# An expert stage whose tokens travel by indirect transfers, with each tile's down product behind the next tile's up products

## The reference

```python
logits = (t @ w_router).astype(F32)
top_v, top_i = lax.top_k(logits, TOP_K)
top_w = jax.nn.softmax(top_v, axis=-1)
gates = jnp.sum(jax.nn.one_hot(top_i, N_EXPERTS) * top_w[..., None], axis=-2)
for e in range(N_EXPERTS):
    out = out + gates[:, e:e + 1] * swiglu(t, w1[e], w3[e], w2[e])
```

## Time and profile before

| | |
|---|---|
| median of 3 runs | 1569.56 us (1569.21 to 1571.90) |
| the profiled execution, its time | 1572.87 us |
| its span | 1571.1 us |
| TensorE busy | 1453.8 us, 93% |
| VectorE busy | 1096.3 us, 70% |
| ScalarE busy | 769.8 us, 49% |
| moved by DMA | 318.02 MB |

### The profile page before, as it was taken

How to read it: one execution, slowest core, us unless ns; L and a number is a source line. 1 busy time by engine, 2 the same in 40 slices (tenths; PEclk the granted TensorE clock), 3 DMA queues, 4 the chain that set the end, 5 groups by cost and what they waited for, 6 DMA issues and landing times.

```text
span 1571.1 us, 19887 instructions
## 1 busy us (share of the span) xinstructions
PE 1453.8 (93%) x7153; PEld 1172.1 (75%) x7153; DVE 1096.3 (70%) x1423; ACT 769.8 (49%) x795; POOL 38.1 (2%) x61
## 2 busy tenths in 40 slices
PE   4999879999999977999999679999999999999996
PEld 1884446999999866778877457787877877877874
DVE  2686975334343467788888648788787787887786
ACT  2420254213222245465655247676676676665662
POOL 1000000000000011000000100000000000000000
PEclk7999989999999987999999879999999999999998
DMA  9888266443433322222223108797897887987971
GB/s 354 306 315 329 107 210 243 167 134 107 133 114 107 106 71 89 85 70 64 83 88 100 55 27 298 274 363 274 280 341 279 304 327 275 349 289 271 350 289 73
DMA packets 136277, 318.02 MB, mean 202 GB/s; under 512 B 5951, under 2 KB 42119, under 8 KB 130087
## 3 DMA queue, kind: packets, MB, share of 16 engines
q1 hardware_dynamic: 132992, 310.14, 55.8%
q0 software_dynamic: 2384, 5.54, 1.1%
q10 hardware_dynamic: 855, 1.74, 0.3%
HBM read 315.63 MB, written 1.77 MB: 202 GB/s over the span
## 4 chain that ended last, share of the span: by engine, by line
PE 80%; DVE 10%; ACT 5%; issue 3%; DVEq 0%; ACTq 0%
PE ps L263 22%; PE ps L265 22%; PE ps L264 22%; DVE v L872 3%; PE ps L1721 3%; PE ps L1606 2%; DVE wl L247 2%; ACT wh L241 2%; PE ps L1332 1%; PE ps L1637 1%; PE ps L1378 1%; PE ps L1610 1%; DVE x L349 1%; DVE yacc L1260 1%; DVE xn L348 1%
## 5 line engine op out<-in xcount | busy, mean ns | idle before, releaser
L247 DVE TENSOR_TENSOR wl<-raw,wh 128x2048 fp32r<-128x2048 f32 x253 | 575.3, 2288 | 150.0 <-ACT wh L241 149.6
L241 ACT ACTIVATE wh<-raw 128x2048 fp32r<-128x2048 f32 x253 | 483.8, 1916 | 292.9 <-PE ps L265 246.7
L263 PE MATMUL ps<-wh,xgh 128*128 128x512 f32 x480 | 193.6, 403 | 10.1 <-DVE yacc L1260 5.1
L265 PE MATMUL ps<-wh,xgl 128*128 128x512 f32 x480 | 190.3, 396 | 0.0
L264 PE MATMUL ps<-wl,xgh 128*128 128x512 f32 x480 | 190.2, 396 | 0.0
L263 PE MATMUL ps<-hTh,wh 128*128 128x384 f32 x480 | 164.6, 343 | 0.0
L264 PE MATMUL ps<-hTl,wh 128*128 128x384 f32 x480 | 163.1, 340 | 0.0
L265 PE MATMUL ps<-hTh,wl 128*128 128x384 f32 x480 | 163.0, 340 | 0.0
L263 PEld LDWEIGHTS ps<-wh,xgh 128*128 128x128 f32 x480 | 90.4, 188 | 35.9 <-issue 8.1
L265 PEld LDWEIGHTS ps<-wh,xgl 128*128 128x128 f32 x480 | 90.4, 188 | 22.0
L264 PEld LDWEIGHTS ps<-wl,xgh 128*128 128x128 f32 x480 | 90.5, 189 | 20.3
(11 more groups left out here) (287 smaller groups left out, 2312.7 us busy)
## 6 DMA issues: line engine op xcount, KB each, us to landing
raw<-in_moe_w SPq DMA_DIRECT2D x180, 1024.0 KB, 6.0
raw<-in_ada_w SPq DMA_DIRECT2D x48, 1024.0 KB, 6.8
raw<-in_ffn_w SPq DMA_DIRECT2D x33, 1024.0 KB, 5.6
raw<-in_conv_pw SPq DMA_DIRECT2D x12, 1024.0 KB, 12.1
raw<-in_mla_wo SPq DMA_DIRECT2D x8, 1024.0 KB, 4.8
raw<-in_mla_wuq SPq DMA_DIRECT2D x8, 768.0 KB, 4.7
gate<-gates_dram POOLq DMA_DIRECT2D x8, 512.0 KB, 4.9
raw<-in_mla_wukv SPq DMA_DIRECT2D x8, 512.0 KB, 3.7
```

The lines of the kernel that those rows point to most:

```text
L241: act.activation(wh[:, split_no(s) % HL, :], raw[:, s % RAW, :], ACT.Copy).then_inc(hi_made, 1)
L247: eng.tensor_tensor(wl[:, split_no(s) % HL, :], raw[:, s % RAW, :], wh[:, split_no(s) % HL, :], ALU.subtract).then_inc(lo_made, 1)
L263: nc.tensor.matmul(out_, sh, mh, start=start, stop=False)
L265: return nc.tensor.matmul(out_, sl, mh, start=False, stop=stop)
```

## The change

* The tokens no longer pass through `sel` in every tile. Two tables in memory, `xs_dram` and `ys_dram`, have a row for each place of 14 tiles. GpSimd writes each token's row to its two places by indirect DMAs (three blocks of tokens, twice), SP loads a tile's 128 rows into `xrow`, and TensorE turns them in eight transposes (`turn_rows_in`). Only tile 0 is still gathered by matmuls. A tile's output goes from PSUM through `ybuf` to `ys_dram`, by a DMA that ScalarE issues (`y_out`). After the last tile, six indirect DMAs bring each token's two rows back, and VectorE weighs and adds them. Scatter, `selT`, `yh`, `yl` and `G` are gone.
* Both tables are filled with zeros in the FFN stage: 28 DMAs of 128 rows, issued by GpSimd. ScalarE waits for them before the norm of the mla stage, since they read `hf`.
* The weights are read as rows of 8 KB. So partition p holds the inputs 8p to 8p + 7, and ScalarE writes `xn` in that order; hidden units are dealt four to a partition, and the product on VectorE writes `hm` in that order. A tile's up chunks are now all of w1 (chunks 0 to 5, banks 0 to 2), then all of w3 (6 to 11, banks 3 to 5). Silu is one instruction over 1536 columns, and the three products stand together.
* The loop is shifted. A turn holds the up chunks of tile e + 1 and the down chunks of tile e; the transposes of the hidden product lie between the first up chunks. Ahead of the loop are 12 up chunks of tile 0, behind it 6 down chunks of the last tile.
* The routing on VectorE makes row numbers (`rows_of`) for the transfers in place of the later tiles' `R` and `G`, in about as many steps.

```diff
+        xs_dram = nc.dram_tensor("xs_dram", [NT * P, D], F32, kind="Internal").ap()
+        ys_dram = nc.dram_tensor("ys_dram", [NT * P, D], F32, kind="Internal").ap()
...
+            ew1, ew3 = (d[n][0].rearrange("e (p k) n -> p e (k n)", k=DK) for n in ("moe_w1", "moe_w3"))
+            ew2 = d["moe_w2"][0].rearrange("e (g p j) n -> p e g (j n)", g=NG, j=4)
...
+            def load_next(e, up_of, down_of, static=False):
+                L = None if static else (e, TILE_CH)
+                load_up(NEXT, ew1, up_of, L)
+                sp.wait_ge(sem("xg_turned"), at(1, None if static else (e, 1)))
+                sp.dma_start(xrow[:, :], xs_dram[2 * P:3 * P, :] if static else xs_dram[ds(e * P + 2 * P, P), :])\
+                    .then_inc(sem("xrow_in"), 16)
+                load_up(NEXT + UP, ew3, up_of, L)
+                load_down(NEXT + 2 * UP, down_of, L)
...
+            load_up(MOE, ew1, 0)
+            load_up(MOE + UP, ew3, 0)
+            sp.wait_ge(sem("dispatched"), 16 * TC * TOP_K)
+            sp.dma_start(xrow[:, :], xs_dram[P:2 * P, :]).then_inc(sem("xrow_in"), 16)
...
+            blank = hf[:, :, :].rearrange("p k t -> p (k t)")[:, 0:D]
+            pool.memset(blank, 0.0).then_inc(sem("blank_made"), 1)
+            pool.wait_ge(sem("blank_made"), 1)
+            for t in range(NT):
+                for table in (xs_dram, ys_dram):
+                    pool.dma_start(table[t * P:(t + 1) * P, :], blank).then_inc(sem("tables_blank"), 16)
+            pool.wait_ge(sem("tables_blank"), 32 * NT)
...
+            pool.wait_ge(sem("rows_made"), 1)
+            pool.wait_ge(sem("tok_made"), TC)
+            for i in range(TOP_K):
+                for c in range(TC):
+                    pool.indirect_dma_start(out=xs_dram[:, :], out_offset=bass.IndirectOffsetOnAxis(ap=rows_of[:, c, i:i + 1], axis=0),
+                                            in_=xn[:, c, :], in_offset=None).then_inc(sem("dispatched"), 16)
...
+            pool.wait_ge(sem("y_last"), 16)
+            for c in range(TC):
+                for i, dst in enumerate((yacc, xn)):
+                    pool.indirect_dma_start(out=dst[:, c, :], out_offset=None, in_=ys_dram[:, :],
+                                            in_offset=bass.IndirectOffsetOnAxis(ap=rows_of[:, c, i:i + 1], axis=0))\
...
+            act.wait_ge(sem("tables_blank"), 32 * NT)
...
+                act.activation(xn[:, c, :].rearrange("p (k b a) -> p b a k", k=DK, b=DK),
+                               ps[:, 2 * c:2 * c + 2, :].rearrange("p u (b a k) -> p (u b) a k", b=DK // 2, k=DK), ACT.Copy)\
...
+            def silu(s, loop):
+                act.wait_ge(chunk_used, at(s, loop))
+                act.activation(ms[:, :, :], ps[:, 0:NG, :], ACT.Silu).then_inc(sem("ms_made"), 1)
...
+            for k in range(2 * UP):
+                make_hi(act, MOE + k + 3)
+                if k == UP:
+                    silu(MOE + UP, None)
+                if k == 11:
+                    rows_hi(xgh[:, :, :], (sem("xg_turned"), 1))
...
+            def y_out(e, s, static, signal):
+                L = None if static else (e, TILE_CH)
+                act.wait_ge(chunk_used, at(s, L))
+                if not static:
+                    act.wait_ge(sem("y_stored"), at(0, (e, 16)))
+                act.activation(ybuf[:, :], ps[:, 6:8, :].rearrange("p a b -> p (a b)"), ACT.Copy).then_inc(sem("y_copied"), 1)
+                act.wait_ge(sem("y_copied"), at(2, None if static else (e, 1)))
+                act.dma_start(ys_dram[0:P, :] if static else ys_dram[ds(e * P, P), :], ybuf[:, :]).then_inc(signal, 16)
+            def tile(e, static=False):
+                L, L1, L3 = (None,) * 3 if static else ((e, TILE_CH), (e, 1), (e, 3))
+                for k in range(TILE_CH):
+                    make_hi(act, NEXT + k + 3, L)
+                    if k in (1, 2, 3):
+                        hidden_hi(k - 1, L3)
+                    if k == UP:
+                        act.wait_ge(sem("hm_made"), at(3, L3))
+                        silu(NEXT + UP, L)
+                    if k == 2 * UP + 2:
+                        rows_hi(xgh[:, :, :], (sem("xg_turned"), at(2, L1)))
...
+            def product(s, L, silu_made, turned=None):
+                dve.wait_ge(sem("ms_made"), silu_made)
+                dve.wait_ge(chunk_used, at(s, L))
+                if turned:
+                    dve.wait_ge(*turned)
+                for g in range(NG):
+                    dve.tensor_tensor(hm[:, g, :].rearrange("p (j r) -> p r j", j=4), ps[:, 3 + g, :].rearrange("p (r j) -> p r j", j=4),
+                                      ms[:, g, :].rearrange("p (r j) -> p r j", j=4), ALU.mult).then_inc(sem("hm_made"), 1)
...
+            for k in range(2 * UP):
+                make_lo(dve, MOE + k + 3)
+                if k == 11:
+                    rows_lo(xgl[:, :, :], xgh[:, :, :], 0, (sem("xg_hi"), 2))
+                    product(MOE + 2 * UP, None, 1)
...
+            def tile(e, static=False):
+                L, L1, L3 = (None,) * 3 if static else ((e, TILE_CH), (e, 1), (e, 3))
+                for k in range(TILE_CH):
+                    make_lo(dve, NEXT + k + 3, L)
+                    if k in (1, 2, 3):
+                        hidden_lo(k - 1, L3)
+                    if k == 2 * UP:
+                        product(NEXT + 2 * UP, L, at(2, L1), (sem("hm_turned"), at(3, L3)))
+                    if k == 2 * UP + 2:
+                        rows_lo(xgl[:, :, :], xgh[:, :, :], 0, (sem("xg_hi"), at(3, L1)))
...
+                dve.wait_ge(sem(f"y_back{c}"), 16 * TOP_K)
+                step(dve.scalar_tensor_tensor(out=yacc[:, c, :], in0=xn[:, c, :], scalar=gap[:, c, 1:2], in1=yacc[:, c, :],
+                                              op0=ALU.mult, op1=ALU.add))
+                step(dve.scalar_tensor_tensor(out=yacc[:, c, :], in0=yacc[:, c, :], scalar=gap[:, c, 3:4],
+                                              in1=gate[:, 1 if c == 0 else 0, :], op0=ALU.mult, op1=ALU.mult))
+                dve.tensor_tensor(x[:, c, :], x[:, c, :], yacc[:, c, :], ALU.add).then_inc(sem("moe_x"), 1)
...
+            def up_chunk(s, i, b, xh, xl, loop):
+                wait_parts(pe, s + i, loop)
+                hi, lo = parts(s + i, 512, 4)
+                for n in range(4):
+                    k, g = (4 * i + n) // NG, (4 * i + n) % NG
+                    last = mm3(ps[:, b + g, :], xh[:, k, :], xl[:, k, :], hi[:, n, :], lo[:, n, :], k == 0, k == DK - 1)
+                last.then_inc(chunk_used, 1)
...
+            def turn_rows_in(silus, rows_):
+                pe.wait_ge(sem("ms_made"), silus)
+                pe.wait_ge(sem("xrow_in"), rows_)
...
+                    last = pe.transpose(ps[:, k // 4, k % 4 * P:k % 4 * P + P], xrow[:, k * P:(k + 1) * P], ident[:, :])
...
+            for i in range(UP):
+                up_chunk(MOE, i, 0, hgh, hgl, None)
+            for i in range(UP):
+                up_chunk(MOE + UP, i, 3, hgh, hgl, None)
+                if i == UP - 2:
+                    turn_rows_in(1, 16)
...
+            def tile(e, static=False):
+                L, L1, L3, L16 = (None,) * 4 if static else ((e, TILE_CH), (e, 1), (e, 3), (e, 16))
+                pe.wait_ge(sem("xg_lo"), at(2, L1))
+                for i in range(UP):
+                    up_chunk(NEXT, i, 0, xgh, xgl, L)
+                    if i < NG:
+                        turn_hidden(i, L3)
+                pe.wait_ge(sem("hg_lo"), at(3, L3))
+                for i in range(UP):
+                    up_chunk(NEXT + UP, i, 3, xgh, xgl, L)
+                pe.wait_ge(sem("y_copied"), at(1, L1))
+                for i in range(2 * NG):
+                    down_chunk(NEXT + 2 * UP, i, L)
+                    if i == 1:
+                        turn_rows_in(at(2, L1), at(32, L16))
...
```

More of the change, by code:

```diff
@@ L152, in hybrid_conv_mla_diffusion_step @@
          (q_sb, qr, KT, QB, pT, oTh, oTl, krh, KR, pr),
-         (yh, yl, sel, selT, ms, R, G, rt, jt, tab, xj, xw, js, upto, lgT, before, iota, router)) = share(
+         (hm, ms, xrow, ybuf, sel, R, rt, jt, tab, xj, js, upto, lgT, before, iota, router, rowf, rows_of)) = share(
             "own",
@@ L818, in _ @@
+            tile(0, static=True)
+            with act.Fori(1, NE - 1) as e:
+                tile(e)
             act.wait_ge(sem("tab_ready"), 1)
@@ L821, in _ @@
                 with act.If(j < more):
-                    heads(j + NE)
-                    tile(j + NE)
+                    tile(j + NE - 1)
+            last = more + NE - 1
+            for g in range(NG):
+                hidden_hi(g, (last, 3))
+            for k in range(3):
+                make_hi(act, NEXT + k + 3, (last, TILE_CH))
+            y_out(last, NEXT + 2 * NG, False, sem("y_last"))
         @block.vector
@@ L1237, in _ @@
[L1237 to L1242 removed]
+            step(dve.tensor_tensor(to, cux.unsqueeze(1).to_broadcast(over), js[:, :, :], ALU.is_le))
@@ L1300, in _ @@
```

(22 more changed lines are left out.)

295 lines of the change are left out of this document (98 added, 197 removed).

## The result

The changed kernel takes 1518.68 us (median of 4 runs, 1517.21 to 1519.81) beside 1569.38 for the kernel before in the same session: a ratio of 0.9666, interval 0.9654 to 0.9678. The forecast was 1518, in a range of 1504 to 1541. The profiled execution took 1519.81 us and has a span of 1518.0.

What follows compares the result with a forecast made beforehand. TensorE was taken to bound each tile. First up product at 940.2 plus 579.5 us (ten bare tiles, row turns, waits, seams, clock, late transfers, tail) gave a 1519.7 span, corrected to 1518 us; range 1504 to 1541.

Steps and rivals of the forecast that it cites:

- Bare tile: Expert stage: a tile's TensorE work without lookups or Silu wait, 18 chunks and three hidden turns, 52.06 us.
- Blanks at no cost: FFN stage: 28 DMAs zeroing the tables, 39 us of full queues, fit under existing work and cost nothing.
- Silu waits: Each tile near up chunk 10: TensorE waits behind table load and Silu of 1536, 0.85 us, 8.5 for ten.
- Late transfers: Expert stage: weight loads that come late cost 0.4 us a tile, 3.6 us over nine tiles.
- The product: Down chunks: three VectorE products of 0.68 us together at k = 12, hidden from TensorE by 0.5 us.
- strided writes rival: Writes of hm and xn 512 bytes apart cost twice: 14 us in nine tiles, 1534 us; chance 0.10.
- Prologue: Before tile(0): splitting tile 1's rows into high and low parts leaves TensorE waiting 5.8 us, once.
- Epilogue: Before the last down product: output copy, issue and hidden copies have no up product over them, 5.4 us.
- Clock: After three gaps (start, prologue, epilogue): lower granted clock costs 1.3 us each, 3.9 in all.
- Tail: Last down matmul to the end: output store, six indirect gathers, weighing rounds and final store, 23.6 us.
- Gathers one by one: Tail rival: the six indirect gathers run one after the other, 41 us for 23.6, 1535 us; chance 0.08.
- The rivals on the transfers: Expert stage: transfers bound the tile at 333 to 364 GB/s, 1523 to 1530 us (0.13), or below 333, 1599 (0.04).

Runs made afterwards that it cites:

- the two loads experiments: Changed kernel with the old kernel's weight loads (2 KB and 4 KB rows): 1518.62 us; kernel before with the changed one's 8 KB-row loads: 1569.87 us.
- exp_silu: Changed kernel with one small Exp ahead of each Silu, so ScalarE loads a table twice per tile: 1544.91 us, ratio 0.9834.
- turn_steps: Changed kernel with VectorE's product in rows at both ends and TensorE's transposes reading hm at a 16-byte step: 1514.91 us, ratio 0.9639.
- the fastest version: Changed kernel with second tile's rows turned earlier, xn written in rows, product in rows with stepped transposes, output copied at k = 9: 1505.55 us, ratio 0.9579.
- before_no_lookup: Kernel before in its own order, gather replaced by 8 transposes, scatter and turn of sel taken out: 1545.42 us, ratio 0.9835.

## Why the prediction was right, and what in it was not

**The mechanism.** TensorE bounds the tile before and after, the lookups leave it, and the tile becomes its bare work: shown by the windows and by the two loads experiments. Bare tile: 52.06 forecast, 51.97 measured (53.14 less row turns 0.79 and the wait 0.38). Row turns 0.9, measured 0.79, and ten of them, not nine. Blanks at no cost: in 250 to 350, where they are written, TensorE is busy for 95.52 us in both kernels, and in 300 to 500 for all of the 200 us.

**Terms that missed, and that met in the sum.** From the first up product to the last down product 555.9 us were forecast and 548.7 measured, 7.2 less.

- Silu waits: 8.5 forecast, 0.8 measured. The step that failed is "Silu of 1536 behind a table load", multiplied by ten. The changed stage has one table load in all, in the prologue, and there chunk 10 does start 0.8 us late, as the forecast's 0.85 says (timeline of the changed kernel):

```profile
964.90 1.28 ACT L832 ACT_TABLE_LOAD   x1
...
971.83 0.50 PE L267 MATMUL ps<-wh,hgh 128*128 128x512 f32 x1 [0.53 <-DVE wl L251]
```

exp_silu puts the loads back in the other tiles and gets the wait back. The kernel before held the hint: its two loads a tile are there 7 times each, in the loop's tiles and not in the three behind it. Its trace even has the price. With the load the first 48 up products and the wait behind them take 12.24 us (at 1065.55 and at 1127.63). In the eighth tile, which has none, the 49th product starts 11.35 us after the first at 1375.91, without a wait:

```profile
1387.25 0.40 PE L263 MATMUL ps<-wh,xgh 128*128 128x512 f32 x1
```

That the loop of before was entered with another table than its end leaves, and the new one is not, fits this; it was argued, not tried.
- Late transfers: 3.6 forecast, none measured.
- The product: hidden in the forecast by 0.5, measured 1.10 us each, 0.38 a tile left bare (11.71 us for 11.33 in turn_steps), 3.4 in nine tiles. The strided writes rival was real at 1.6 times the old length, not twice, and cost a quarter of its 14 us. The xn copies, taken "at their old length", took 1.9 times that: 2.0 of the 2.7 us by which the first up product came late (942.91 for 940.2).
- Prologue 5.8 forecast, 5.52 measured. Epilogue 5.4 forecast, 6.40 measured: between the output's issue and its hidden copies ScalarE stands 2.1 us at the end of the loop, which I had left out (timeline of the changed kernel):

```profile
1466.56 1.00 ACT L857 ACTIVATE ybuf<-ps 128x1024 f32<-128x1024 f32 x1
1467.73 0.35 ACTq L859 DMA_DIRECT2D ys_dram<-ybuf  x1
1469.67 1.57 ACT L837 ACTIVATE hgh<-ps 128x512 fp32r<-128x512 f32 x3 [2.11 <-issue]
```

- Clock: 1.3 us a gap forecast from one gap of 2.37 us; the gaps of 5.5 and 6.4 cost 2.3 (12 up products in 5.08 us for 2.81) and 2.2. Behind the gap at the start, which the forecast priced too, this profile has clock 1.00. So 4.5 us stand against 3.9.
- Tail: 23.6 forecast, 26.4 measured. The store was done 4.8 us after the last product, as forecast (1496.42), and the rounds took 3.77 each. The landing of the gathers was mis-sized: the first pair was there 7.1 us after its first issue, not 4.5. Gathers one by one fell: they overlap at 1.26 us apart.

**The rivals on the transfers.** Both fall. The rate rose to 370 and 376 GB/s with both engines reading raw, 381 in the fastest version, and nothing waited for raw. The Trainium skill, DMA: Bandwidth & Descriptors, section Bandwidth, gives some 358 GB/s for each core when both of a pair stream, and says that a lone core measured more. The trace agrees for a lone core, with 366 held over 525 us; no run here has both cores at work.

So the forecast's 1518 was better than its terms, and that it came within 1 us is luck. Some 12 us too much (Silu 7.7, transfers 3.6, bare tiles, row turns and the prologue's gap 0.9) stood against some 10.5 too little (product 3.4, tail 2.8, start 2.7, epilogue 1.0, clock 0.6): a span of 1518.0 for 1519.7. The last step was luck as well. The forecast took off 3.3 us because the profiled execution of before lay that far above its median; here it lay 1.1 above, so a span 1.7 us too long became a median 0.5 us too short. What the forecast had right is the part that decides the sign and most of the size: which work leaves TensorE, and that the copies and the transfers can follow at a period near 53 us.

## What to carry to other kernels

Work taken off the bounding engine is worth only what does not return as an uncovered hand-over: here 1.8 of 9.1 us a tile in the mean, until the order gave the copies something to lie behind. Count, for the engine that feeds the bound, every microsecond between two chunks, and look in which tiles an overhead such as a table load really stands before multiplying it by all of them. A gap at a seam costs its length and the clock behind it, so a copy done two chunks earlier can be worth more than any edit inside the loop.

## What the hardware showed unexpectedly

- Waits of the same 2.05 us at the same place in nine tiles lowered the granted clock behind four of them (0.64 to 0.73 over 3 us, 1.5 us lost each) and left it at 1.00 behind the others. Waits of 3.91 us in before_no_lookup lost 1.4 and 2.4 us by turns. What tells them apart stays open.
- Queues at share 0.98 to 0.99 over hundreds of microseconds, and no wait for a transfer: the busy share alone did not show a transfer bound.
- TensorE transposes that read float32 at a step of 16 bytes took 280 ns for 272, where VectorE's product at such steps took 1085 for 682.
- GpSimd issues an indirect DMA of 128 rows of 4 KB in 0.95 us, 1.26 apart.
